# Softmax attentions in steps of two heads on partition halves: one transformer pair on one Trainium2 core

## The reference, cut to what matters

```python
# first block, layer 0: 8 heads of 64; 512 local keys (banded by rows and columns, with a bias) and 256 context keys
s_loc = where(mask, q_r @ k_r * scale + bias, NEG_INF); s_ctx = q_r @ k_ctx * scale
p = softmax(concat([s_loc, s_ctx])); o = p_loc @ v_r + p_ctx @ v_ctx
yc_b = gqa_attend(qc, kc, vbc)                 # and the 256 context tokens on themselves, 8 heads
# layer 1: 16 query heads of 64 over 4 key heads, 768 keys (512 and the context)
s = einsum(qg, k) * dh**-0.5; p = softmax(s); o = p @ v
# second block, each of two layers
o_b = swa_attention(q, k, v, pos, sinks, rel)  # 6 heads of 64, window of 128: 128 to 256 keys, bias, sink
o_a = mla_attention(q, k, v)                   # 6 heads of 96, causal: 128, 256, 384 or 512 keys for the four query tiles
o_c = stick_breaking_attention(q, k, v)        # 4 heads; not changed
```

## Time and profile before

| | |
|---|---|
| median of 3 runs | 4774.35 us (4774.03 to 4783.82) |
| the profiled execution | 4777.86 us, of which its span is 4776.1 us |
| PE busy over the span | 4137.6 us |
| DVE, ACT, POOL busy | 2275.3, 1465.4, 1623.7 us |
| A0, from the first scores on | 368.6 to about 556 us |
| A1 | 1471.0 to about 1732 us |
| SWA, MLA, MLA of the second block's first layer | 2836.7 to 2902, 2943.4 to 2971, 3007.9 to 3036 us |
| the same of its second layer | 4098.2 to 4163, 4203.1 to 4230, 4267.5 to 4295 us |

### The profile page before, as it was taken

The page is one execution under the profiler, slowest core; times in us unless marked ns, Lnnn a source line. Parts: engine busy times, 40 slices in busy tenths (PEclk is TensorE's granted clock), DMA queues, the critical chain, the costliest instruction groups (busy, mean ns, idle before and its releaser), DMA issues. The chain is left out here.

```text
span 4776.1 us, 49724 instructions
## 1 busy us (share of the span) xinstructions
PE 4137.6 (87%) x17588; PEld 3028.7 (63%) x17588; DVE 2275.3 (48%) x3833; ACT 1465.4 (31%) x2329; POOL 1623.7 (34%) x804
## 2 busy tenths in 40 slices
PE   1698879999868998997999778789989988877998
PEld 0683458888654455885887543468868866425886
DVE  4656686553445466664453845531232232464122
ACT  1124332222223433333222244332222223443221
POOL 0220024444231014564544300245545543014553
PEclk9898789999988998998999877899989989788999
DMA  6151014442110013671664110023323321101332
GB/s 194 42 152 30 25 44 133 132 141 83 31 49 9 1 38 117 228 226 60 216 228 142 52 31 26 27 71 101 93 66 93 96 70 53 35 0 49 97 93 65
DMA packets 459948, 410.67 MB, mean 86 GB/s; under 512 B 29983, under 2 KB 404895, under 8 KB 459807
## 3 DMA queue, kind: packets, MB, share of 16 engines
q1 hardware_dynamic: 447728, 400.53, 27.0%
q10 hardware_dynamic: 12079, 8.33, 0.6%
HBM read 405.14 MB, written 7.60 MB: 86 GB/s over the span
## 5 line engine op out<-in xcount | busy, mean ns | idle before, releaser
L198 POOL TENSOR_TENSOR s_wlo<-s_raw,s_whi 128x1024 fp32r<-128x1024 f32 x490 | 1183.2, 2422 | 2145.0 <-ACT s_whi L190 2145.0
L212 PE MATMUL psum<-s_xhi,s_whi 128*128 128x512 f32 x3264 | 1250.8, 383 | 192.1 <-POOL s_xlo L509 139.0
L213 PE MATMUL psum<-s_xlo,s_whi 128*128 128x512 f32 x3264 | 1238.4, 379 | 0.0
L214 PE MATMUL psum<-s_xhi,s_wlo 128*128 128x512 f32 x3264 | 1234.6, 378 | 0.0
L190 ACT ACTIVATE s_whi<-s_raw 128x1024 fp32r<-128x1024 f32 x490 | 510.2, 1055 | 1947.2 <-PE psum L214 1917.6
L212 PEld LDWEIGHTS psum<-s_xhi,s_whi 128*128 128x128 f32 x3264 | 625.0, 191 | 348.4 <-issue 131.8
L214 PEld LDWEIGHTS psum<-s_xhi,s_wlo 128*128 128x128 f32 x3264 | 625.1, 192 | 116.3
L213 PEld LDWEIGHTS psum<-s_xlo,s_whi 128*128 128x128 f32 x3264 | 626.9, 192 | 110.4 <-issue 2.6
L212 PE MATMUL psum<-s_ahi,s_whi 128*128 128x512 f32 x1232 | 476.7, 387 | 32.3 <-POOL s_wlo L198 22.7
L833 DVE TENSOR_TENSOR s_y<-s_y,psum 128x512 f32<-128x512 f32 (+1 forms) x528 | 376.0, 730 | 256.6 <-PE psum L214 245.8
L213 PE MATMUL psum<-s_alo,s_whi 128*128 128x512 f32 x1232 | 473.8, 385 | 0.0
(11 more groups left out here) (212 smaller groups left out, 4579.0 us busy)
## 6 DMA issues: line engine op xcount, KB each, us to landing
s_ada_raw<-w_ada SPq DMA_DIRECT2D x224, 512.0 KB, 3.8
s_raw<-w_gu SPq DMA_DIRECT2D x176, 512.0 KB, 3.9
s_raw<-w_up SPq DMA_DIRECT2D x88, 512.0 KB, 4.7
s_raw<-w_dn SPq DMA_DIRECT2D x88, 512.0 KB, 3.3
s_raw<-w_down SPq DMA_DIRECT2D x44, 512.0 KB, 4.5
s_raw<-w_in SPq DMA_DIRECT2D x28, 512.0 KB, 3.9
s_raw<-w_in_ab SPq DMA_DIRECT2D x20, 512.0 KB, 5.4
s_area<-w_ada SPq DMA_DIRECT2D x16, 512.0 KB, 10.0
```

Of the source, the lines that this page charges most:

```text
L198: pool.tensor_tensor(K.wlo[:, c % HL, 0:a * b], K.raw[:, c % RAW, 0:a * b], K.whi[:, c % HL, 0:a * b].bitcast(F32), ALU.subtract).then_inc ...
L212: pe.matmul(out, lh, rh, start=first, stop=False)
L213: pe.matmul(out, lh, rl, start=False, stop=False)
L214: return pe.matmul(out, ll, rh, start=False, stop=last)
```

## The change

`Attn` now works in steps of a query tile and two heads (in MLA still one head, since its heads have 96 rows). The two heads of a step lie on the two partition halves for queries and keys, and their outputs go to the two halves of one bank. Values are made for each step, 128 query columns at a time, in place of once for a head. The transposes of a step go in chunks of four blocks through one bank, so each chunk waits until the one before it has been copied out; in A0 and A1 a step has 12 blocks and three chunks. Scores run two steps ahead in all phases, and their buffers are two steps deep. For 768 keys the scores of the two heads share a middle bank and are issued in two halves. DVE adds the bias and takes the maximum in one instruction; the scale is folded into queries and gains; the tables of the biased heads are made on GpSimd, up to four heads ahead. The core of the diff:

```diff
-        for u in range(self.lead):
-            scores(u)
-        for u, (h, t) in enumerate(self.units):
-            if u + self.lead < len(self.units):
-                scores(u + self.lead)
-            if h > 0:
-                values(h - 1, t, len(self.heads[h].units))
-            transposes(u)
-        values(len(self.heads) - 1, 0, 1)
+        def scores(s, half):
+            t = self.steps[s][1]
+            w, k0 = self.n(s) * P, self.keys(s)[0] * P
+            pieces = [(0, 512, 256), (1, 256, 512), (0, 0, 512), (1, 0, 256)] if w == T0 else [
+                (j, 0, w) for j in range(self.nh(s))]
+            if half == 0 and s >= 2:
+                e.wait_ge(self.sem["p_exp"], self.at("p_exp", self.ub[s - 1]))
...
+        def transposes(s, c):
+            blocks = [(j, b) for j in range(self.nh(s)) for b in range(self.n(s))][4 * c:4 * c + 4]
+            e.wait_ge(self.sem["p_ready"], self.at("p_ready", self.ub[s] + blocks[-1][0] + 1))
+            e.wait_ge(self.sem["t_copied"], self.at("t_copied", self.cb[s] + c))
...
+        def values(s):
...
+            for b, kt in enumerate(keys):
+                for j, (_, _, v) in enumerate(self.group(s).heads):
+                    ins = e.matmul(self.o(g, j)[:, t * P:(t + 1) * P], v(kt), self.pt(s, j * len(keys) + b),
+                                   start=(b == 0), stop=(b == len(keys) - 1))
...
+        for s in range(n):
+            chunks = self.cb[s + 1] - self.cb[s]
+            transposes(s, 0)
+            if s > 0:
+                values(s - 1)
+            if chunks > 1:
+                transposes(s, 1)
+            if s + 2 < n:
+                scores(s + 2, 0)
+            if chunks > 2:
+                transposes(s, 2)
+            if s + 2 < n:
+                scores(s + 2, 1)
...
+        exp(0)
+        for s in range(n):
+            if s + 1 < n:
+                exp(s + 1)
+            for c in range(self.cb[s + 1] - self.cb[s]):
+                copy(s, c)
+                if c == 0 and s > 0 and self.last(s - 1):
+                    output(s - 1)
...
+            e.wait_ge(self.sem["s_ready"], self.at("s_ready", self.ub[s + 1]))
...
+                    e.tensor_tensor_reduce(out=x[:, 0:w], in0=x[:, 0:w], in1=bias, scale=1.0, scalar=first, op0=ALU.add,
+                                           op1=ALU.max, accum_out=m).then_inc(K.sem["dve_step"], 1)
...
+        for s in range(min(2, n)):
+            top(s)
+        for s in range(n):
+            normal(s)
+            if s + 2 < n:
+                top(s + 2)
+            if s > 0 and self.last(s - 1):
+                output(self.steps[s - 1][0])
...
+    def pool(self, e):
+        bias = self.bias
+        for i in range(bias.n if bias else 0):
...
+            bias.prepare(e, i).then_inc(self.sem["e_ready"], 1)
```

More of the change, by code:

```diff
@@ L948, in pool, with __init__ @@
                                      ALU.subtract).then_inc(self.sem["mix_lo"], 1)
[L951 to L962, removed]
-class Attn(Phase):
[L970 to L979, removed]
+class Heads:
+    def __init__(self, heads, tiles, out, half=0, biased=False, diag=False, sinks=None):
+        self.heads, self.tiles, self.out, self.half = heads, tiles, out, half
+        self.biased, self.diag, self.sinks = biased, diag, sinks
@@ L980, in __init__ @@
         super().__init__(K)
-        self.e0, self.ada_read = K.e_loads, K.ada_tasks
-        K.e_loads += sum(hd.load is not None for hd in heads)
+        self.ada_read = K.ada_tasks
     def counts(self):
[L985 to L990, removed]
@@ L1013, in complete @@
[L1013 to L1020, removed]
+        n = self.ub[-1]
+        c = dict(s_ready=n, nm_ready=n, p_exp=n, p_ready=n, t_ready=self.cb[-1], t_copied=self.cb[-1],
+                 pv_ready=len(self.steps), o_hi=sum(isinstance(g.out, tuple) for g in self.groups),
+                 o_done=len(self.groups))
@@ new lines, in counts, with group, nh, keys @@
+        c["s_shared"] = sum(self.n(s) == 6 for s in range(len(self.steps)))
+        if self.bias:
+            c["e_ready"] = self.bias.n
+            for i in range(self.bias.n):
+                c[f"e_in{i % self.bias.raws}"] = c.get(f"e_in{i % self.bias.raws}", 0) + 32
+        return c
+    def group(self, s):
+        return self.groups[self.steps[s][0]]
+    def nh(self, s):
+        return len(self.group(s).heads)
+    def keys(self, s):
+        g, t = self.steps[s]
+        return self.groups[g].tiles[t]
@@ L1022, in sp @@
     def sp(self, e):
-        K, i = self.K, self.e0
+        K, bias = self.K, self.bias
         self.ahead(e)
[L1025 to L1039, removed]
+        if not bias:
+            return
@@ L1058, in transposes @@
-        def transposes(u):
-            h, t = self.units[u]
-            blocks = self.heads[h].units[t]
-            e.wait_ge(self.sem["p_ready"], self.at("p_ready", u + 1))
-            e.wait_ge(self.sem["t_copied"], self.at("t_copied", self.tb[u]))
[L1063 to L1066, removed]
@@ L1134, in outputs @@
             if isinstance(out, tuple):
[L1135 removed]
+                e.activation(out[0], self.o(g), ACT.Copy).then_inc(self.sem["o_hi"], 1)
             else:
[L1137 to L1144 removed]
@@ L1145, in act @@
-        outputs(len(self.heads) - 1)
+                e.activation(out, self.o(g), ACT.Copy).then_inc(self.sem["o_done"], 1)
+        exp(0)
[6 more added lines that the diff above has]
+                    output(s - 1)
+        output(n - 1)
     def dve(self, e):
-        K = self.K
+        K, n = self.K, len(self.steps)
@@ L1213 @@
+        output(self.steps[n - 1][0])
 class HeadNorm(Phase):
@@ L1757, in build @@
     K = Keep()
[L1758 removed]
+    K.nc, K.io, K.total, K.phases, K.chunks, K.ada_tasks, K.steps = nc, io, {}, [], [], 0, 0
     K.loaded = 0
```

386 lines of the change are left out of this document (185 added, 201 removed).

## The result

The changed kernel takes 4976.4 us (4974.9 to 4979.0, four runs) against 4774.2 (4772.2 to 4783.8, four runs of the same chip): 1.042 times as long, 95% interval 1.0402 to 1.0438. It is slower by 202 us. The prediction said 5090 (4900 to 5210), so 316 us more than before, and the measured loss is 64% of that. The profiled execution has a span of 4973.1 us against 4776.1.

A forecast was written before the change was run, and what follows sets the result against it. PE's stream nearly bounds A1 and A0, a chain between engines SWA and MLA; the change makes steps serial. A1 +83, A0 +52, context heads +3, MLA +145, SWA +34 total +317: 4774.4 + 317 = 5090 us, range 4900 to 5210.

The forecast's parts named there:

- the forecast case: Whole kernel: PE and DVE take turns in a serial step, clock mixed or low, 4980 to 5200 us; chance 0.65.
- A0 with its context heads: A0: local heads 16 steps of 11.6 us against 134 us, +52; context heads 8 steps of about 5.6, +3.
- the four MLA: MLA: one head a step, nothing paired, lower clock, 57.7 us a phase against 21.4, +36 each, +145 for four.
- the two SWA: SWA: 12 steps of two heads, 6.4 us each or 5.5 with 128 keys, 74 against 57, +17, twice +34.
- The step at the full clock: A1: one serial step of two heads of 768 keys sums to 8.24 us, 8.4 with the output subtraction.
- paired values: A1's step: 24 value passes run as 12 pairs, 1.28 + 0.17 us; the passes alone would be 2.57 unpaired.
- The third rival: Whole kernel: serial step and short matmuls do not pair, A1 +102, A0 +51, total 5240 us; chance 0.07.
- The clock in A1: A1: mixed clock gives 10.6 us a step, 32 steps 339 us against 256, +83 (+13 to +154).
- Half of the time at each level: PE's clock: half the time full, half lower, taken between 1.00 and 0.92 and 0.56 and 0.50; A1's step 10.6 us.
- The ends of a phase: All phases: values of one step at the end, where before they were of a whole head; costed at nothing.
- The fourth rival: Faster: PE's streams bound, A1's step 5.5 us, A1 176 us (-80), A0 -38, SWA -5 each, total 4645; chance 0.09.
- the move of the last split's wait: Phases: this wait moves from head to end, costed at nothing; each late table would cost about 2 us.

The follow-up runs named there:

- the two unpaired runs: Scores first with one head's value matmuls all ahead of the other's, 4650.7 us; the same with wide-step score matmuls also one head after the other, 4648.6 us.
- scores first: The changed kernel with PE issuing both halves of scores(s+2) ahead of transposes(s) in every phase: 4604.8 us, 0.962 to 0.9659 of the kernel before.

## Why the prediction was right, and where it was off

**Sign and mechanism** were right: each row it named is there. The size was not: +202 us against +316, inside the range but 4 us below the band of the forecast case (4980 to 5200), and every large term was too high. A1 was +38 for +83, A0 with its context heads +26 for +55, the four MLA +109 for +145, the two SWA +13 for +34; the 10 us outside the series stood nowhere. Reciprocals of A1 come in pairs 8.1 to 11.2 us apart, DVE waits for the scores and PE for the scaling in every step, PE's busy time falls, MLA phases take 46 to 48 us. The runs show the cause from three sides: undoing PE's order alone removes the loss, breaking the ring on DVE removes most of it in MLA and all of it in SWA, and the order alone, put into the kernel before, makes a loss in SWA and MLA.

**The step at the full clock**, 8.24 us for A1 before the output, measured 8.08, and paired values 1.28 + 0.17 = 1.45, measured 1.46 (1642.73 to 1644.19). The third rival (no pairing) falls, by the trace and the two unpaired runs.

**The clock in A1** is the largest miss. "Half of the time at each level" gave 10.6 us a step; the window shows 0.83, which is a third of the time at the lower level ((1 - 0.83) / 0.5 = 0.34), and apart from the last the steps take 9.6 us in the mean, 9.65 most often. Two things are in this miss. First, 10.6 is the mean of a step at the full clock and one at the lower; half of the *time* at each level is 1 / (0.5 / 8.4 + 0.5 / 12.8) = 10.1 us a step. Second, the share. A lower stretch costs only where PE works in it, and in most steps it lies on the first transposes and the values:

```profile
1651.00 2.83 PE L1109 MATMUL psum<-s_area 128*64 128x128 f32 x24
```

These 24 passes take 2.83 us where the step before took 1.53; with 0.19 and 0.08 more for the transposes on either side that is the 1.57 between 8.08 and 9.65. Steps with a group's output take 0.6 more at the full clock (8.68), which is 0.15 a step. No row of before could fix the share; I put it halfway. In the series A1 is +38 where the term was +83: 1 us a step is 32 of the 45.

**The ends of a phase** were costed at nothing, and that was the second miss, in the other attentions the main one. MLA was to be +36 a phase. A cycle of four tiles takes 3.92 + 5.18 + 5.33 + 4.89 = 19.32 us, where 19.3 stood in the prediction, at the clock taken, 0.50; DVE's part of 1.40 against 1.50 and 0.79 for changes of kind and ways against 0.64 cancel. But the first step has no values yet (3.14) and the last no scores or maxima (0.93), so the series is 47.6 us and not twelve full steps, 57.7. Against the 19.6 of before that is +28 (the sum took 21.4 for before, 1.8 more than its series). The same in A1 (last step 1.45) is some 8 us, and in SWA (1.31) some 4.

**A0** was to be +52 for the local heads. From their first reciprocal to the first of the context heads 169.6 us pass (133.5 before), so sixteen steps took 10.6 us each instead of 11.6, +36. The lower level held half of the time here (0.73 to 515 us), as taken. At the full clock a step would be A1's 8.08 and 1.0 for the fused maxima (both heads' take 2.75 us in the trace, A1's 1.74), 9.1, not 9.4. So the lower level added 1.5 us a step where 2.1 stood. The context heads' series is 10 us shorter (33.2 for 43.2), where +3 stood.

**SWA** was to be +17 each, measured +7 and +6. A cycle of four tiles takes 5.59 + 5.71 + 5.46 + 6.15 = 22.9 us, 5.7 a step and not 6.2: DVE's part lasts 2.48 us (2931.76 to 2934.24) to 2.75 (2943.22 to 2945.97) and not 2.95, since the two heads' small operations run into each other. One step in each SWA takes 8.19 us, for a reason that the prediction left at nothing when it moved the tables to GpSimd:

```profile
2924.83 1.26 POOL L2014 TENSOR_TENSOR s_h<-s_ada_acc,s_before 128x512 f32<-128x512 f32 x1 [9.89 <-DVE s_stat L1197]
2924.99 1.25 DVE L1214 TENSOR_SCALAR s_t<-s_t,s_stat 128x256 f32<-128x256 f32 x1
```

While GpSimd makes tables, DVE's scaling of 256 columns takes 1.25 us, where it takes 0.35 at 2919.27, and the addition of the sink to a sum, one column, behind it 1.21 instead of 0.15. The table is not late, but its making slows DVE, by some 2.6 us in each SWA.

**The fourth rival** put the streams' bound at 5.5 us a step and A1 at 176 us, if DVE made the maxima of s+2 while PE transposes s. Exactly that edit gives 5.53 and 173.5. It was not what the change did, but the same arithmetic said what one move in the order would bring. Its estimates elsewhere were short: SWA -5 each against -21 and -22, A0's local heads -38 against -48; MLA, left unchanged there, is 1 to 3 us longer.

**Costed at nothing**: the move of the last split's wait. In A0 the first reciprocal comes at 377.2 (below), as in the earlier trace rows (377.1), so it holds there. What the attentions' ends and the stretches between them add, some 10 us, I had not foreseen and didn't pursue. The source line of the reciprocal after the change, A0 with its context heads and A1:

```profile
L1212 DVE RECIPROCAL s_stat<-s_stat x48: 151/154/157, 377.2 to 580.1; 128x1 f32<-128x1 f32 x48
L1212 DVE RECIPROCAL s_stat<-s_stat x64: 152/155/163, 1504.6 to 1794.8; 128x1 f32<-128x1 f32 x64
```

## What to carry to other kernels

Write the order of each in-order queue beside the others' and look for a ring: if the step ahead is issued behind work that waits for an engine, whose own queue holds the step ahead in front of that work, the two never overlap, however little each has to do. A better layout of the work shows only after the order is right: with paired heads and late scores the kernel lost 202 us, with scores first it gained 169, and 46 of these are the paired values. Breaking a ring where its first link is (PE's scores) was worth twice as much (372 us against 169) as breaking it one engine on, where the next queue (ACT) closed it again.

## What was unexpected of the hardware

Passes on the two partition halves overlap though four passes of one head are issued before any of the other (1.57 us for eight passes, of which the columns alone would be 2.56 one after another); with twelve of each in a row only four of each overlap (2.46 us for 24 passes of 0.107, 1.53 when they alternate).

An added matmul of 384 columns in each step raised the granted clock from 0.50 to 0.86 and made the kernel 47 us faster: a phase of short waits pays for PE's idleness a second time.

While GpSimd works on a table of 512 columns, DVE's scaling of 256 columns in SBUF takes 1.25 us instead of 0.35, and its addition of a single column 1.21 instead of 0.15; its reciprocal keeps its 0.16 (2927.41).
